# Sliding attention of a two-part block: interleaved projections, and units of one query block with two heads and the mask on TensorE

## The reference, cut to what matters

```
q, k, v = split(a @ w_qkv)           # 16 query heads, 4 key heads, width 64
q, k = rms_norm per head, then rotary (latent tokens only; k of the 256 context tokens is not rotated)
for each block of 128 queries:
    s = q . [k of the window, k of the context] / 8
    s = where(|qpos - kpos| <= 128 or context, s, -1e30)
    m = max(max(s), sink);  e = exp(s - m)
    p = e / (sum(e) + exp(sink - m));  o = p @ [v, v of context]
y = heads side by side @ w_o
```

## Time and profile before

| what | value |
|---|---|
| median of 3 runs | 2245.79 us (2243.2 to 2246.06) |
| the profiled execution, its own time | 2239.34 us |
| its span, first to last instruction | 2237.5 us |
| TensorE busy, share of the span | 92%, mean granted clock 0.957 |
| VectorE, ScalarE busy | 38%, 17% |
| Q chunk 0 starts, projections end | 1375.7 us, 1433.8 us |
| first scores | 1480.4 us |
| output projection starts | 1587.5 us |

### The profile page before, as it was taken

One profiled execution on the slowest core, in us unless ns is written; L12 is line 12 of the kernel. 1 busy time (PEld: TensorE's weight loads), 2 busy tenths in 40 slices (PEclk: granted clock), 3 DMA queues, 4 the chain that ended last, 5 costly groups with the idle time before them and its releaser, 6 DMA issues.

```text
span 2237.5 us, 40982 instructions
## 1 busy us (share of the span) xinstructions
PE 2052.2 (92%) x18732; PEld 1763.0 (79%) x18732; DVE 855.6 (38%) x1431; ACT 379.1 (17%) x693; POOL 14.9 (1%) x10
## 2 busy tenths in 40 slices
PE   7989889999998989889999999858899999999999
PEld 4778578799997778578899997524688888878878
DVE  4767683200005748553200003266466501113320
ACT  3021412000002022411000003124211101012110
POOL 0000000000000000000000000000000000000000
PEclk8999989999999999989999999979999999999999
DMA  9991564399993662453599993200288734434420
GB/s 360 387 340 62 183 226 191 123 367 384 397 395 144 223 223 94 151 184 122 187 360 383 401 388 113 81 0 0 75 286 281 271 123 149 151 113 151 143 102 19
DMA packets 184179, 466.03 MB, mean 208 GB/s; under 512 B 5153, under 2 KB 55681, under 8 KB 176385
## 3 DMA queue, kind: packets, MB, share of 16 engines
q1 hardware_dynamic: 183776, 463.83, 56.5%
q10 hardware_dynamic: 288, 0.52, 0.1%
HBM read 463.29 MB, written 1.05 MB: 208 GB/s over the span
## 4 chain that ended last, share of the span: by engine, by line
PE 81%; DVE 12%; ACT 3%; issue 3%; DMA 1%; SPq 0%; DVEq 0%; ACTq 0%
PE pair L359 80%; DVE AR L1472 1%; DMA ring<-in_ada_w 1%; DVE SM L2004 1%; DVE AR L1975 1%; ACT AR L1357 1%; ACT AR L1196 1%; DVE AR L1689 1%; DVE RST L1527 1%; DVE AR L2002 0%; DVE XH L1472 0%; DVE AR L2003 0%; DVE AR L1699 0%; SPq L250 0%; PE pair L860 0%
## 5 line engine op out<-in xcount | busy, mean ns | idle before, releaser
L359 PE MATMUL pair<-XH,ring 128*128 128x256 f32 (+4 forms) x3584 | 816.5, 390 | 21.4 <-ACT XH L1099 17.3
L359 PE MATMUL pair<-AR,ring 128*64 128x96 f32 (+1 forms) x12992 | 808.5, 262 | 29.3 <-issue 15.2
L359 PEld LDWEIGHTS pair<-AR,ring 128*64 128x64 f32 (+1 forms) x12992 | 761.0, 143 | 75.0 <-issue 22.1
L359 PEld LDWEIGHTS pair<-XH,ring 128*128 128x128 f32 (+3 forms) x3584 | 684.3, 192 | 137.5 <-issue 28.3
L1942 DVE TENSOR_TENSOR AR<-AR,pair 128x384 f32<-128x384 f32 x30 | 16.6, 554 | 449.9 <-PE pair L359 449.9
L1472 DVE SCALAR_TENSOR_TENSOR AR<-ring,CACT,AR 128x512 f32<-128x512 f32 x245 | 184.2, 752 | 8.7
L359 PE MATMUL pair<-AR 128*128 128x128 f32 (+6 forms) x640 | 139.9, 385 | 20.0 <-ACT AR L1370 15.5
L359 PEld LDWEIGHTS pair<-AR 128*128 128x128 f32 (+3 forms) x640 | 90.9, 183 | 61.6 <-ACT AR L1370 28.1
L1559 DVE SCALAR_TENSOR_TENSOR XH<-pair,MOD,XH 128x256 f32<-128x256 f32 x64 | 28.3, 480 | 214.6 <-PE pair L359 214.5
L2036 DVE SCALAR_TENSOR_TENSOR AR<-pair,VEC,AR 128x255 f32<-128x255 f32 x88 | 41.9, 476 | 114.6 <-ACT AR L1395 114.6
L1301 ACT ACTIVATE AR<-pair 128x768 f32 x30 | 24.5, 815 | 306.1 <-PE pair L359 306.1
(11 more groups left out here) (248 smaller groups left out, 1124.8 us busy)
## 6 DMA issues: line engine op xcount, KB each, us to landing
ring<-in_ada_w SPq DMA_DIRECT2D x48, 2048.0 KB, 12.7
ring<-in_w_gate SPq DMA_DIRECT2D x32, 2048.0 KB, 9.1
ring<-in_w_up SPq DMA_DIRECT2D x32, 2048.0 KB, 9.4
ring<-in_w_down SPq DMA_DIRECT2D x32, 2048.0 KB, 9.5
ring<-in_ffn_w_up SPq DMA_DIRECT2D x44, 1024.0 KB, 7.6
ring<-in_w_in SPq DMA_DIRECT2D x18, 2048.0 KB, 12.1
ring<-in_ffn_w_down SPq DMA_DIRECT2D x8, 2048.0 KB, 8.5
ring<-in_sc_w_in SPq DMA_DIRECT2D x6, 2048.0 KB, 7.9
```

The lines of the kernel that those rows point to most:

```text
L359: return pe.matmul(o, lhsT, rhs, start=start, stop=stop, **kw)
```

## The change

Projections, norm and rotary: the order on PE becomes Q0, K tile 0, square sums of Q0, K tile 1, Q1 tile 0, sums of K, Q1 tile 1, rotation of Q0, Q1 tiles 2 and 3, V tile 0, sums of Q1, rotation of K, V tiles 1 and 2, the copying of K, rotation of Q1, V tile 3. ACT and DVE take the three chains in the order Q0, K, Q1. Squares go to blocks 2 and 3, roots to 10 and 11, and each rotation goes to the PSUM pair that its tile came from. The counts of Q1 and of the last chunk are given later in the order.

Attention: a unit is `(t, b)`, query block b with both heads 2t and 2t+1. Scores are one product per head, each on its own half of the rows and in its own bank, followed by two products of the identity with a 128 x 128 part of the mask, added in PSUM. DVE takes the maximum straight from PSUM, ACT the exponential straight from PSUM with the scale 1/8 in it, and DVE normalises with two tensor_scalar. The values are eight products of 128 columns that alternate between the two halves of the output columns. DVE's order becomes max(0), max(1), then normalise(u), max(u+2). PE's becomes scores(0), scores(1), then for each u scores(u+2), values(u-1), transposes(u). Scores(u+2) now wait for ACT's exponential of unit u in place of DVE's maximum. The core of the diff:

```diff
-        WNM, WRS, WES = [SM[:, 8 * i:8 * i + 8].rearrange("p (a n) -> p a n", a=2) for i in range(3)]
+        WNM, WRS, WES, WMX, WNS = [SM[:, 8 * i:8 * i + 8].rearrange("p (a n) -> p a n", a=2) for i in range(5)]
+        NSINK = SM[:, 40:56]
...
-        wq_copied wsum_ready wstd_ready wn_ready wrot_ready wroped k_dup kdup_copied wv_copied
+        wk_made wq_copied wsum_ready wstd_ready wn_ready wrot_ready wroped k_dup kdup_copied wv_copied
...
-            for k, q in enumerate((PA, PB)):
-                done(features(ck("wqkv", k), [half(q, m) for m in range(4)], lambda t: H2[:, t, 0:S],
-                              first=5 if k == 0 else None))
+            QT, QP = [blk(0), blk(4), blk(1)], [PA, PC, PB]
+            def wq_tile(c, q, m, first=None):
+                w = view(c, KT, 512)
+                for t in range(KT):
+                    if first is not None:
+                        h_tile(first, t)
+                    last = mm(half(q, m), w[:, t, m * P:m * P + P], H2[:, t, 0:S], t == 0, t == KT - 1)
+                return last
+            def wk_tile(m):
+                w = view(ck("wqkv", 2), KT, 512)
+                for t in range(KT):
+                    last = mm(PC[:, 512 * m:512 * m + 512], w[:, t, m * P:m * P + P], H2[:, t, :], t == 0, t == KT - 1)
+                return last
+            def wv_tile(m):
+                w = view(ck("wqkv", 2), KT, 512)
+                for t in range(KT):
+                    last = mm(PD[:, S * m:S * m + S], H2[:, t, m * P:m * P + P], w[:, t, 256:512], t == 0, t == KT - 1)
+                return last
+            def wsums(i):
+                pe.wait_ge(s["wsq_ready"], i + 1)
+                for m in range(2):
+                    last = mm(QP[i][:, 512 * m:512 * m + 512], cB, blk(2 + i % 2)[:, 512 * m:512 * m + 512], True, True)
+                last.then_inc(s["wsum_ready"], 1)
+            def wrotated(i):
+                pe.wait_ge(s["wn_ready"], i + 1)
+                n = S if i == 1 else 512
+                for m in range(2):
+                    last = mm(QP[i][:, n * m:n * m + n], cP, QT[i][:, 512 * m:512 * m + n], True, True)
+                last.then_inc(s["wrot_ready"], 1)
+            arrived(ck("wqkv", 0))
+            for m in range(4):
+                last = wq_tile(ck("wqkv", 0), PA, m, 5 if m == 0 else None)
+            done(last)
             arrived(ck("wqkv", 2))
             for t in range(KT):
                 h_tile(5, t, 1)
...
+            wk_tile(0)
             wsums(0)
...
+            wk_tile(1).then_inc(s["wk_made"], 1)
+            arrived(ck("wqkv", 1))
+            wq_tile(ck("wqkv", 1), PB, 0)
+            wsums(1)
+            wq_tile(ck("wqkv", 1), PB, 1)
+            wrotated(0)
+            wq_tile(ck("wqkv", 1), PB, 2)
+            done(wq_tile(ck("wqkv", 1), PB, 3))
+            wv_tile(0)
+            wsums(2)
+            wrotated(1)
+            wv_tile(1)
+            wv_tile(2)
+            pe.wait_ge(s["wroped"], 2)
...
-                last = mm(o, sel, QT[2][:, 512 * (g // 2):512 * (g // 2) + 512], True, True)
+                last = mm(o, sel, QT[1][:, 512 * (g // 2):512 * (g // 2) + 512], True, True)
             last.then_inc(s["k_dup"], 1)
+            wrotated(2)
+            done(wv_tile(3))
+            pe.wait_ge(s["wroped"], 3)
...
-            units = [(t, k) for t in range(8) for k in range(2)]
+            WMASK = CS[:, C1_OVER + D_WM:C1_OVER + D_WM + 512]
             def wscores(u):
-                t, kind = units[u]
-                g = t // 2
+                t, b = u // 2, u % 2
                 o = (PA, PB)[u % 2]
                 if u >= 2:
-                    pe.wait_ge(s["sm_max"], 3 * DEPTH + u - 1)
-                lo = 64 * kind
-                for b in range(2):
-                    last = mm(o[:, 512 * b:512 * b + 512], Q2[lo:lo + 64, t, b * P:b * P + P],
-                              KDUP[lo:lo + 64, g, :], True, True)
+                    pe.wait_ge(s["sm_exp"], 3 * DEPTH + u - 1)
+                for k in range(2):
+                    mm(o[:, 512 * k:512 * k + 512], Q2[64 * k:64 * k + 64, t, b * P:b * P + P],
+                       KDUP[64 * k:64 * k + 64, t // 2, :], True, False, skip_group_check=True)
+                edge = P * (1 - b)
+                for k in range(2):
+                    last = mm(o[:, 512 * k + edge:512 * k + edge + P], ident, WMASK[:, S * b + edge:S * b + edge + P],
+                              False, True, skip_group_check=True)
                 last.then_inc(s["sc_ready"], 1)
-            def wweighted(u):
-                t, kind = units[u]
-                g = t // 2
+            def wturned(u):
                 pe.wait_ge(s["p_ready"], 3 * DEPTH + u + 1)
                 if u >= 1:
                     pe.wait_ge(s["pt_ready"], 3 * DEPTH + u)
                 pr = blk(12 + u % 2)
                 for m in range(8):
-                    src = pr[:, (m % 2) * 512 + (m // 2) * P:(m % 2) * 512 + (m // 2) * P + P]
-                    last = pe.transpose(PC[:, m * P:m * P + P], src, ident)
+                    last = pe.transpose(PC[:, m * P:m * P + P], pr[:, m * P:m * P + P], ident)
                 last.then_inc(s["p_turned"], 1)
-                if u + 2 < 16:
-                    wscores(u + 2)
+            def wapplied(u):
+                t, b = u // 2, u % 2
                 pe.wait_ge(s["pt_ready"], 3 * DEPTH + u + 1)
                 pt = blk(14 + u % 2)
-                o = PD[:, 512 * (t % 2):512 * (t % 2) + 512]
-                if kind == 0 and t >= 2:
+                o = PD[:, 512 * (t % 2) + P * b:512 * (t % 2) + P * b + P]
+                if b == 0 and t >= 2:
                     pe.wait_ge(s["ot_copied"], t - 1)
-                for k in range(4):
-                    last = mm(o[64 * kind:64 * kind + 64, 0:S], WV[:, k, g * 64:g * 64 + 64],
-                              pt[:, S * k:S * k + S], k == 0, k == 3)
+                for kb in range(4):
+                    for k in range(2):
+                        last = mm(o[64 * k:64 * k + 64, :], WV[:, kb, 64 * (t // 2):64 * (t // 2) + 64],
+                                  pt[:, (4 * k + kb) * P:(4 * k + kb) * P + P], kb == 0, kb == 3)
                 last.then_inc(s["ot_ready"], 1)
...
-                wweighted(u)
+                if u + 2 < 16:
+                    wscores(u + 2)
+                if u >= 1:
+                    wapplied(u - 1)
+                wturned(u)
+            wapplied(15)
...
+            QT, QP = [blk(0), blk(4), blk(1)], [PA, PC, PB]
+            for i in range(3):
+                if i == 1:
+                    act.wait_ge(s["wk_made"], 1)
+                else:
+                    multiplied(ck("wqkv", i // 2))
+                A(QT[i], QP[i], ACT.Copy).then_inc(s["wq_copied"], 1)
+                act.wait_ge(s["wq_copied"], i + 1)
+                A(blk(2 + i % 2), QT[i], ACT.Square).then_inc(s["wsq_ready"], 1)
+                act.wait_ge(s["wsum_ready"], i + 1)
+                if i == 2:
+                    act.wait_ge(s["wn_ready"], 1)
+                A(blk(10 + i % 2), QP[i], ACT.Sqrt, scale=1.0 / WHD, bias=EPSC[:, 0:1]).then_inc(s["wstd_ready"], 1)
             act.wait_ge(s["k_dup"], 1)
             A(blk(5), PA, ACT.Copy)
             A(blk(6), PC, ACT.Copy).then_inc(s["kdup_copied"], 1)
+            multiplied(ck("wqkv", 2))
+            A(blk(7), PD, ACT.Copy).then_inc(s["wv_copied"], 1)
             def wsoft(u):
                 act.wait_ge(s["sm_max"], 3 * DEPTH + u + 1)
+                if u >= 2:
+                    act.wait_ge(s["p_turned"], 3 * DEPTH + u - 1)
                 pr = blk(12 + u % 2)
-                for b in range(2):
-                    A(pr[:, 512 * b:512 * b + 512], pr[:, 512 * b:512 * b + 512], ACT.Exp,
-                      bias=WNM[:, u % 2, b:b + 1], accum_out=WRS[:, u % 2, b:b + 1])
-                A(WES[:, u % 2, 0:2], WNM[:, u % 2, 0:2], ACT.Exp,
-                  bias=VEC[:, V_SINK + u:V_SINK + u + 1]).then_inc(s["sm_exp"], 1)
+                for k in range(2):
+                    A(pr[:, 512 * k:512 * k + 512], (PA, PB)[u % 2][:, 512 * k:512 * k + 512], ACT.Exp, scale=float(WHD ** -0.5),
+                      bias=WNM[:, u % 2, k:k + 1], accum_out=WRS[:, u % 2, k:k + 1])
+                A(WES[:, u % 2, 0:2], WNS[:, u % 2, 0:2], ACT.Exp).then_inc(s["sm_exp"], 1)
...
+            QT, QP = [blk(0), blk(4), blk(1)], [PA, PC, PB]
+            for i in range(3):
+                gcol, std = (V_WQ, V_WK, V_WQ)[i], blk(10 + i % 2)
+                V.wait_ge(s["wstd_ready"], i + 1)
                 link(V.reciprocal(std, std))
-                V.scalar_tensor_tensor(QT[u], QT[u], VEC[:, gcol:gcol + 1], std, ALU.mult, ALU.mult).then_inc(s["wn_ready"], 1)
...
+                V.wait_ge(s["wrot_ready"], i + 1)
+                n = 2 if i == 1 else 4
+                q = QT[i].rearrange("p (t n) -> p t n", t=n)[:, :, 0:S]
                 t_ = blk(9, n * S).rearrange("p (t n) -> p t n", t=n)
```

(71 more changed lines are left out.)

35 lines of the change are left out of this document (2 added, 33 removed).

## The result

The changed kernel takes 2167.45 us at the median (2164.49 to 2172.88, 4 runs) against 2245.93 us before (2243.2 to 2246.37, 4 runs): a ratio of 0.9656, 95% interval 0.9635 to 0.9677, or 77 us less (72 to 82). The forecast was 2178.7, the range 2163 to 2194. The profiled execution took 2172.88 us, its span is 2171.1.

The account below looks back on a forecast made before the run. DVE's reciprocals bound norm and rotary, and its in-order queue around ACT's exponential bound the loop. Gains of 32.6 us (projections) and 34.5 us (loop), 67.1 in all, take 2245.79 to 2178.7 us; range 2163 to 2194.

Parts of the forecast that it names:

- Part 1: Projections with norm and rotary chains between them: first scores 55.3 us after Q0 instead of 87.9, a gain of 32.6 us.
- my bound for late hand-offs: Projections: two of three rotations have under 1 us of slack, so late hand-offs cost up to 3 us.
- The bound of the old loop: Old attention loop, 6.11 us per unit: bound by DVE's in-order queue with ACT's 1.52 + 0.20 us inside it.
- The loop: Attention: PE binds at 4.17 us per unit; 72.6 us from first scores instead of 107.05, a gain of 34.5 us.
- three slots of 0.43: Scores on PE: second pass of one head runs beside first pass of the other, 1.28 us for the pair.
- cheaper PE: Rival, loop: scores wholly side by side or cheaper shape changes, 6 to 15 us less, 2164 to 2173; chance 0.20.
- The row that I took for the nearest: Sixteen earlier records, taken as alternating between column halves, 1.14 us with their end; basis for overlap of scores and values.
- Changes of shape: Loop on PE: each change of product shape costs 0.16 us; three new ones make 0.48 per unit.
- The rings behind PE: Loop: waits around two rings, 2.9 and 2.7 us per unit with two units in flight, below PE's 4.17.
- row halves that don't overlap: Rival, loop: scores 1.71, unit 4.60 us, 2184.7; 2196 if values gained nothing either; chance 0.16.
- chains that aren't hidden: Rival: level hand-offs in the projections slip and PSUM reads are slower than priced; some 4 us, 2183; chance 0.10.
- the fallen clock: Rival, loop: small gaps hold the clock at half, without overlap unit 10.2 us, kernel 2266, slower than before; chance 0.03.

Follow-up runs that it names:

- longer chain: Changed kernel with one more, unused 6.55 us reciprocal on VectorE ahead of K's: first scores 64.8 us after Q0, loop 67.2 us, 2175.07 us in all.
- unit-by-unit run: Changed kernel, but VectorE does maximum and normalising of one unit before beginning the next: loop 78.5 us, 2176.98 us in one run.
- doubled scores: Changed kernel with each unit's score products made twice, order 0, 1, 0, 1 or 0, 0, 1, 1: loop 78.5 and 78.6 us.
- values in twos: Changed kernel with the eight value products in head order 0, 0, 1, 1, 0, 0, 1, 1: loop 66.4 us, 2172.35 us in all.
- grouped orders: Changed kernel with scores made twice in order 0, 0, 1, 1: loop 78.6 us; or with values four per head in turn: loop 73.4 us.
- mask on VectorE: Changed kernel without the two mask products; VectorE adds the mask in PSUM instead: loop 58.8 us, 2161.57 us, ratio 0.9635.
- projections only: Changed kernel with the loop's code on PE, ACT and DVE put back to that of before: 2208.81 us, ratio 0.9843.
- loop only: Changed kernel with the projections put back to those of before: loop 67.2 us, 2198.87 us, ratio 0.9795.

## Why the prediction was right, and where not

**Part 1** came out as summed: 55.4 for 55.3 us, and step by step, so it wasn't luck. The three reciprocal-and-multiply pairs ended 17.7, 37.2 and 48.5 us after Q0 where the sum has 17.6, 37.3 and 48.7. The prices were K's chunk per product and DVE's own rows, and the hand-offs of K and Q1 are as level as stated. The longer chain shows that they have no more than 0.4 us to give, and that my bound for late hand-offs, up to 3 us, left out the clock: a wait of 6.2 us cost 9.4.

**The bound of the old loop**, DVE's in-order queue with the exponential inside, is shown by the unit-by-unit run: put back alone, it brings DVE's wait back and 0.66 us per unit. The forecast for that run, 4.7, was 0.3 too long: its three pieces took 1.56, 1.57 and 1.28 with their hand-offs, where it had 1.6, 1.6 and 1.35 and 0.15 on top.

**The loop** was right in kind (PE binds, never waits, clock 1.00; DVE and ACT wait) and 7.0 us too long, 72.6 for 65.6. By pieces of a unit:

| PE, start to start | forecast | measured |
|---|---|---|
| scores to mask | 1.28 + 0.16 | 1.06 |
| mask to values | 0.43 + 0.16 | 0.64 |
| values to transposes | 0.96 + 0.16 | 1.02 |
| transposes to scores | 1.02 | 1.02 |
| unit | 4.17 | 3.75 |

The step that was mis-sized is "in order the second pass of one head can run beside the first of the other: three slots of 0.43". The first passes of both heads start together: 0.86 for the pair, as the doubled scores show. That is the whole 0.42 of a unit; the mask with its change (0.05 more) and the values (0.10 less) about cancel with the rest. Thirteen units make 13 x 0.42 = 5.5 of the 7.0 us; the other 1.5 are 0.5 each until the first exponential is done, in the first unit, and in the last two. My rival "cheaper PE" had this at 6 us, and the measured 2167.45 lies in its band, 2164 to 2173, to which I gave 0.20.

The row that I took for the nearest spoke against that step, and I misread it. The sixteen records of 1.14 us at 284.22 in the earlier trace rows don't alternate product by product. They come from a loop over four heads with two products each, so in twos, and the values in twos take the same 1.14 with their end. By my pass order such groups would overlap only at their edges, and the sixteen would have taken 13 slots of 0.11, 1.4 us. On the scores the Trainium skill, TensorE: Matmul & The Clock Gate, Measured speedup vs the span model, was nearer than I was: a packed group lasts about one matmul. The same page says under The mechanism, in Part 3, that matmuls start and end strictly in program order. The grouped orders don't bear this out across halves: four score products in the order 0, 0, 1, 1 take 1.92 us as in the order 0, 1, 0, 1, which leaves room only if the second head's records start beside the first head's, ahead of their turn. The measurement decides.

**Changes of shape**: the row gave 0.16 a piece, and they cost 0.14 to 0.20. The rule that a change of tiling mode drains the engine (the Trainium skill, TensorEngine Tiling (Array Packing), Key Properties) agrees with the sign; as an objection to mixed units it weighs under 0.2 us a time.

**The rings behind PE** were summed too low. With two units in flight I had 2.9 and 2.7 us (the first sum, 2.1 + 1.7 + 1.7, halves to 2.75), and DVE's 3.1 as the next limit. The mask on VectorE brought out one that I had left out: PE's order lets only one unit be between transposes and values, and that ring is 3.23.

**Three rivals are out**: row halves that don't overlap (unit 4.60), chains that aren't hidden, and the fallen clock (10.2). For the last, the longer chain shows its mechanism at work; the new loop has no such wait, and its granted clock was 1.00. In the unit-by-unit run, where PE waits 0.59 us in each unit, the clock was 1.00 too from the first scores on for 72 us.

**The total** was 11.3 us too high at the median: 7.0 from the loop, the rest within the scatter of the untouched parts. The medians of projections only, loop only and the changed kernel, taken side by side (ratios 0.9843, 0.9795, 0.9653), give gains of 35, 46 and 78 us, 3 to 6 above what the stages show. The kernel before itself had medians of 2246.17, 2238.99 and 2245.7 beside the three sets of experiments, with runs from 2234.78 to 2250.44 beside the second. The clock is likely a part of this: before the end of Q0 the traces show it at its lower level for 113 to 130 us in all, longer on the whole where Q0 ended late (112.6 us where it ended at 1389.4, 129.7 at 1401.2, but 116.1 at 1397.3). Why it falls at other places in some executions, and whether that is all, stays open.

## What to carry to other kernels

When an engine's in-order queue holds a wait for another engine's answer, put the next unit's first half ahead of it: two units in flight were worth 0.66 us of 4.41 even after everything else had been made cheaper. Count a long wait of TensorE, like the 6.2 us here, twice, once as time and once as the clock behind it. Before a row is taken for the nearest, read in the code in which order its records were issued. And after each such step write down the next ring (here transposes, copy, values), because it stood only 0.5 us below the one that was removed.

## What the hardware showed that I had not expected

- Two float32 products of 64 rows and 512 columns on different row halves take 0.86 us together, as long as one; a second pair adds 0.86, in either order.
- The side-by-side run reaches beyond neighbours: groups of four records per half hide almost wholly (1.08 us, against 1.02 alternating), of eight by half (1.51).
- A piece of another shape costs PE 0.14 to 0.20 us more, 0.09 of it before its first record; a piece of the same shape follows without a gap (0.11 from record to record across it).
- Adding a 256-column mask in place in PSUM costs DVE 0.43 us, and makes this kernel's loop 6.8 us shorter than the mask's 0.64 us per unit on TensorE.
- A wait of 6.2 us on TensorE was followed by 7 us at a granted clock of 0.59.
